# Attention scores on TensorE: the low queries meet only the high keys, in 64 rows, the two key halves on the array's two row halves

## What is computed

```
q = rmsnorm(q.reshape(b, s, H_B, HEAD_DIM), qn_g)      # 8 heads of 64
k = rmsnorm(k.reshape(b, s, KV_HEADS, HEAD_DIM), kn_g) # 2 key heads
v = v.reshape(b, s, KV_HEADS, HEAD_DIM)
q = apply_axial_rope(q, tables)
k = apply_axial_rope(k, tables)
scale = HEAD_DIM ** -0.5
...
sc = jnp.einsum('bqkgd,bskd->bkgqs', qblk, k).astype(jnp.float32) * scale
p = jax.nn.softmax(sc, axis=-1).astype(v.dtype)
return jnp.einsum('bkgqs,bskd->bqkgd', p, v)
```

## Time and profile before

| | us |
|---|---|
| median of 3 runs | 2312.51 (2309.94 to 2312.78) |
| the profiled execution | 2307.94 |
| its span, first to last instruction | 2306.2 |
| TensorE busy in the span | 2268.0 (98%) |
| VectorE busy | 1077.0 (47%) |
| ScalarE busy | 888.5 (39%) |
| scores' matmuls, lines 961 and 962, 256 each | 103.3 and 100.8 busy |

### The profile page before, as it was taken

The page is one execution under the profiler, slowest core; times in us unless marked ns, Lnnn a source line. Parts: engine busy times, 40 slices in busy tenths (PEclk is TensorE's granted clock), DMA queues, the critical chain, the costliest instruction groups (busy, mean ns, idle before and its releaser), DMA issues.

```text
span 2306.2 us, 28550 instructions
## 1 busy us (share of the span) xinstructions
PE 2268.0 (98%) x11640; PEld 1919.1 (83%) x11640; DVE 1077.0 (47%) x1439; ACT 888.5 (39%) x1426; POOL 274.0 (12%) x276
## 2 busy tenths in 40 slices
PE   8999999999999999999999999998999999999998
PEld 7887799988888789998788898887888888888887
DVE  4313399954333259983624152325334344342343
ACT  5222477744322257772444141323212222222232
POOL 0097200000029600000013020000000000000000
PEclk9999999999999999999999999999999999999999
DMA  6111000033311000003311101322111121124232
GB/s 202 37 55 37 1 1 1 1 137 120 92 46 55 19 1 1 1 22 113 141 59 42 60 19 37 118 66 91 47 55 52 39 55 46 45 98 149 92 127 73
DMA packets 104210, 141.48 MB, mean 61 GB/s; under 512 B 11670, under 2 KB 65094, under 8 KB 104102
## 3 DMA queue, kind: packets, MB, share of 16 engines
q1 hardware_dynamic: 104102, 139.97, 18.4%
HBM read 123.18 MB, written 16.78 MB: 61 GB/s over the span
## 4 chain that ended last, share of the span: by engine, by line
PE 94%; DVE 3%; ACT 1%; issue 1%; DMA 0%; DVEq 0%; SPq 0%; ACTq 0%
PE ps L199 24%; PE ps L201 24%; PE ps L200 24%; PE ps L974 5%; PE ps L989 3%; PE ps L990 3%; PE ps L961 2%; PE ps L962 2%; PE ps L938 1%; PE ps L228 1%; PE ps L925 1%; PE ps L275 1%; PE ps L1953 1%; PE ps L675 1%; DVE hT_lo L290 1%
## 5 line engine op out<-in xcount | busy, mean ns | idle before, releaser
L199 PE MATMUL ps<-w_hi,hT_hi 128*128 128x512 f32 (+1 forms) x1760 | 678.5, 386 | 2.4 <-DVE hT_lo L238 1.4
L201 PE MATMUL ps<-w_hi,hT_lo 128*128 128x512 f32 (+1 forms) x1760 | 672.0, 382 | 0.0
L200 PE MATMUL ps<-w_lo,hT_hi 128*128 128x512 f32 (+1 forms) x1760 | 671.6, 382 | 0.0
L183 DVE TENSOR_TENSOR w_lo<-w_raw,w_hi 128x2048 fp32r<-128x2048 f32 x89 | 207.6, 2333 | 539.4 <-ACT w_hi L167 536.8
L199 PEld LDWEIGHTS ps<-w_hi,hT_hi 128*128 128x128 f32 x1760 | 331.2, 188 | 66.8 <-issue 2.1
L201 PEld LDWEIGHTS ps<-w_hi,hT_lo 128*128 128x128 f32 x1760 | 331.1, 188 | 64.7
L200 PEld LDWEIGHTS ps<-w_lo,hT_hi 128*128 128x128 f32 x1760 | 331.4, 188 | 62.5 <-issue 0.5
L167 ACT ACTIVATE w_hi<-w_raw 128x2048 fp32r<-128x2048 f32 x71 | 135.9, 1914 | 502.2 <-PE ps L201 502.2
L199 PE MATMUL ps<-hT_hi,w_hi 128*128 128x512 f32 x832 | 324.2, 390 | 5.0 <-DVE X L2523 2.7
L201 PE MATMUL ps<-hT_hi,w_lo 128*128 128x512 f32 x832 | 323.7, 389 | 0.0
L200 PE MATMUL ps<-hT_lo,w_hi 128*128 128x512 f32 x832 | 323.7, 389 | 0.0
(11 more groups left out here) (203 smaller groups left out, 2363.3 us busy)
## 6 DMA issues: line engine op xcount, KB each, us to landing
w_raw<-in_ffn_w_up SPq DMA_DIRECT2D x44, 512.0 KB, 5.0
w_raw<-in_ffn_w_down SPq DMA_DIRECT2D x22, 1024.0 KB, 4.9
w_raw<-in_w_in SPq DMA_DIRECT2D x21, 1024.0 KB, 5.1
x_mid<-X SPq DMA_DIRECT2D x24, 512.0 KB, 2.7
w_raw<-in_gla_w_in SPq DMA_DIRECT2D x12, 1024.0 KB, 5.1
X<-in_x SPq DMA_DIRECT2D x16, 512.0 KB, 7.1
w_raw<-in_w_out SPq DMA_DIRECT2D x8, 1024.0 KB, 6.7
X<-x_mid SPq DMA_DIRECT2D x16, 512.0 KB, 7.4
```

What stands on the lines that cost most here:

```text
L183: engine.tensor_tensor(self.p.w_lo[:, slot, 0:size], self.p.w_raw[:, slot, 0:size], plane(self.p.w_hi[:, slot, 0:size]), ALU.subtract).the ...
L199: nc.tensor.matmul(out, a_hi, b_hi, start=first, stop=False)
L200: nc.tensor.matmul(out, a_hi, b_lo, start=False, stop=False)
L201: return nc.tensor.matmul(out, a_lo, b_hi, start=False, stop=last)
```

## The change

The two products with the high queries stay as they are. The two with the low queries are cut to 64 rows each: for the first 512 keys `QT_lo` in partitions 0 to 63 with the high keys in partitions 0 to 63 of `KT_st`; for the last 512 keys `QT_lo` in partitions 64 to 127 with a copy of the high keys in partitions 64 to 127, the new tile `KT_up`. Each writes its own PSUM bank, and each still makes 128 queries by 512 keys. The product of low queries and low keys is left out of the scores. The order within a tile becomes high, high, low, low. The high keys of the last 512, which were scratch in `KT_hi`, now stay in `KT_up`; the scratch of the first 512 goes into a part of `QT_hi` that is not yet in use.

```
-        self.KT_hi = prog.at("KT_hi", [P, SEQ], kb + 88, F32R)
+        self.KT_up = prog.at("KT_up", [P, KV, SEQ // 2], kb + 88, F32R)
...
+    def low_keys(self, i):
+
+        return self.KT_up[HD:P, i // 2, :] if i % 2 else self.QT_hi[HD:P, 1, 0:SEQ // 2]
...
+            g, tok = head // (H_B // KV), slice(t * P, (t + 1) * P)
             for half in range(2):
-                keys = self.KT_st[:, head // (H_B // KV), half * 512:(half + 1) * 512]
-                out = prog.ps[:, 2 * (n % 2) + half, :]
-                nc.tensor.matmul(out, self.QT_hi[:, head % 2, t * P:(t + 1) * P], keys, start=True, stop=False)
-                mm = nc.tensor.matmul(out, self.QT_lo[:, head % 2, t * P:(t + 1) * P], keys, start=False, stop=True)
-            mm.then_inc(self.s_ready, 1)
+                nc.tensor.matmul(prog.ps[:, 2 * (n % 2) + half, :], self.QT_hi[:, head % 2, tok],
+                                 self.KT_st[:, g, half * 512:(half + 1) * 512], start=True, stop=False)
+            nc.tensor.matmul(prog.ps[:, 2 * (n % 2), :], self.QT_lo[0:HD, head % 2, tok],
+                             self.KT_st[0:HD, g, 0:512], start=False, stop=True)
+            nc.tensor.matmul(prog.ps[:, 2 * (n % 2) + 1, :], self.QT_lo[HD:P, head % 2, tok],
+                             self.KT_up[HD:P, g, :], start=False, stop=True).then_inc(self.s_ready, 1)
...
-            nc.scalar.activation(self.KT_hi[HD:P, cols], prog.ps[HD:P, self.turn_bank(i), :], ACT.Copy
+            nc.scalar.activation(self.low_keys(i), prog.ps[HD:P, self.turn_bank(i), :], ACT.Copy
...
-                                    plane(self.KT_hi[HD:P, i % 2 * 512:(i % 2 + 1) * 512]), ALU.subtract
+                                    plane(self.low_keys(i)), ALU.subtract
```

## The result

The changed kernel takes 2324.97 us (median of 6 runs, 2321.93 to 2327.11), the kernel before, run beside it, 2309.99 us (2309.94 to 2312.78). The ratio is 1.0063, 95% interval 1.0052 to 1.0074: 15 us slower. The forecast was 2329 us in a range of 2306 to 2357, slower with a chance of 0.65.

A forecast was written before the change was run, and what follows sets the result against it. The prediction took TensorE to bound the attention. A loss of 0.17 us in 128 tiles, 21.8 us, less 4.8 absorbed, left 17.0; added to the median of 2312.5 this gave 2329 us, range 2306 to 2357.

The forecast's parts named there:

- The bound: Attention is bound by TensorE, busy 98% of the span, with a slack of 0.24 us in 28 of 128 tiles.
- Way in, 0.32: From the start of the second full matmul to the first narrow load: 0.32 us, as at the 44-row transposes.
- The narrow loads, 0.06 + 0.06: The two 64-row weight loads in a tile, one after the other: 0.06 us each, bounds 0.06 and 0.11.
- Way out, 0.32: From the second narrow matmul's start to the transposes' load: 0.32 us, bounds 0 and 0.32, not shown for this direction.
- The transposes' first load, 0.11: The 128-row load of line 974 after the narrow pair, in the open: 0.11 us.
- Absorbed in 28 tiles: Where line 938 waits 0.24 us anyway, the 0.17 us loss is absorbed: 28 x 0.17 = 4.8 us.
- The sum: Per tile 0.87 us against 0.70, loss 0.17; 128 tiles lose 21.8 us, less 4.8 absorbed, leaving 17.0.
- The signs: Expected in the profile after: narrow and transpose load gaps, head's stretch about 26.2 us, line 938's pieces about 0.46, full clock.
- Full overlap: Rival: the narrow pair runs at once with no wait, saving 0.23 us a tile; -23, 2290 us; chance 0.21.
- a serial pair: Rival: both waits, and the second narrow matmul starts 0.23 us behind the first; +37, 2349 us; chance 0.2.
- the free change of shape: The no-wait part of the rival at 2290 us, chance 0.21: the 0.32 at 1600 us has another cause.

The follow-up runs named there:

- 96-row run: Against the kernel before: both low-query products on the first 96 partitions, in the order high, high, low, low; 2312.12 us, ratio 1.0006.
- run in full rows: Against the changed kernel: new order and key places kept, both low-query products back to 128 rows; 2310.01 us, ratio 1.0000 to the kernel before.
- run with both on one half: Against the changed kernel: the second narrow product also reads partitions 0 to 63, as the first does; 2350.51 us, ratio 1.0175 to the kernel before.
- run with four changes: Against the changed kernel: same four products in the order high, low, high, low; 2398.44 us, ratio 1.0396 to the kernel before.

## Why the prediction was right

- **The bound.** Right: TensorE carried the chain, and what was put on it came out in the time, but for the first tiles of each layer (below).
- **Way in, 0.32.** Measured 0.33. The single instance at the 44-row transposes was read rightly as the shape change: a cause of its own at that place, such as new code, can't stand in all 128 tiles, and the 96-row run and the run in full rows exclude the number of rows and the order. The Trainium skill (TensorEngine Tiling (Array Packing), Key Properties) says that changing the mode drains the engine and changing the tile does not; the traces agree on both, 0.33 and 0.01 us.
- **The narrow loads, 0.06 + 0.06.** Wrong twice, and it cancelled. An open load of 64 rows takes 0.11 (second pair behind the first, 383.43 to 383.54), and the two loads of a pair don't queue, they run beside each other. 0.11 for both against 0.12.
- **Way out, 0.32.** Measured 0.43 - 0.11 = 0.32. In the run with both on one half the second narrow matmul's start stands by itself, and the next load comes 0.32 behind it (394.91 to 395.23). It had no row before; that both directions cost the same was an assumption, it decided between slower and no change, and it held.
- **The transposes' first load, 0.11.** This is the term that was mis-sized, and with it the loss of a tile. I took 0.87 / 8 = 0.11 as the time of a load, but it is the time of the transpose that hides it. With the array empty, two loads stand in 0.20 us of which one takes 0.14, so 0.06 apart. The tile's loss is 0.33 + 0.11 + 0.32 + 0.06 - 0.70 = 0.12 by these terms, 0.13 from the chain, and not 0.17.
- **Absorbed in 28 tiles.** Right: 0.24 of wait became 0.13, and the head's stretch grew by 0.78 = 6 x 0.13, not by 8 x 0.13. Not in the forecast: the first tiles of a layer have slack too. There TensorE of the kernel before waits in some places anyway, in the second layer once 2.1 us for an exponential ahead of line 961. From the first score of that layer, at 832.10 and 840.83, to that of its eighth tile, before and after:

```profile
851.04 0.40 PE L961 MATMUL ps<-KT_st,QT_hi 128*128 128x512 f32 x1
```

```profile
859.92 0.63 PE L964 MATMUL ps<-KT_st,QT_hi 128*128 128x512 f32 x2
```

That is 18.94 and 19.09 us, 0.15 more, where five steps that don't turn a head would pay 0.65.

- **The sum.** 100 tiles by 0.13 are 13.0 us; with 0.5 a layer off for the first tiles, 12.0; the two layers' stretches, which leave out the last tile, show 11.4. The forecast had 17.0. The clock added some 3 us to the median, which was not in the sum; that 17 is so near the measured 15 is in part luck. Of the 4 us between 2329 and 2324.97 the base has 2.5: the forecast started from 2312.5, the median of three runs, and six runs beside the changed kernel gave 2309.99.
- **The signs.** The loads of lines 966 and 968 stood as forecast, 0.33 and 0.01. The load of line 980 was to stand 0.3 behind the start of line 968 and stands 0.42 behind it in the rows, which print a narrow matmul and its open load at the same start; less the 0.11 of that load it is about as forecast. The head's stretch was to be 26.2 and is 25.98, line 942's pieces 0.46 and are 0.52. Wrong were the full clock throughout and that the rest of the program would take the same: in this trace it takes 6.0 us more, by the stretches at half the clock.
- **The rivals.** Full overlap was right (chance given to a serial pair: 0.2), the free change of shape was wrong. The pair does save a whole matmul, 0.23 us a tile; the two changes of shape cost 0.36.

## What to carry to other kernels

Two 64-row matmuls on the two row halves do run as one, but a change of the array's shape and back costs about one and a half 512-column matmuls here (0.36 against 0.23 us); so it takes more than one pair between two changes, and the work for that must be there without making another engine late. A forecast by tiles is checked by tiles: the head's stretch and the layer's stretch told more than the median, which has the clock in it. Look for the one odd-shaped instruction that the kernel already has: its gap priced this change before it ran. A spacing of 0.11 us in a row of loads says how far apart they are, not how long one takes; look at what it hides behind before pricing it in the open.

## What was not expected of the hardware

- The loads of the two row halves start within 0.01 us of each other and take no longer together than one (0.43 us from the first load to the next full one with a pair, and with a single narrow matmul in the run with four changes).
- The wait beyond the matmul's own spacing is 0.08 to 0.10 us: 0.08 after 256 columns and 0.10 after 512 on the way in, 0.09 (0.32 - 0.23) on the way out.
- A full matmul that follows a narrow one pays the same as the other way round; 96 rows pay nothing.
